# Four consecutive keys per partition: a cache page as 32 rows of 8 KB instead of 128 rows of 2 KB

## What is computed

```python
past_k = cache_k[l][page_table].reshape(dec_batch, past_len, DA_HEADS, 2, DA_HEAD_DIM)
past_v = cache_v[l][page_table].reshape(dec_batch, past_len, DA_HEADS, 2 * DA_HEAD_DIM)

def _da_decode(q, k_new, v_new, past_k, past_v, lam):
    s_past = jnp.einsum("bqhmd,bshmd->bhmqs", q, past_k).astype(jnp.float32)
    s_new = jnp.einsum("bqhmd,bshmd->bhmqs", q, k_new).astype(jnp.float32)
    ...
    a = _diff_map(jnp.concatenate([s_past, s_new], axis=-1), lam).astype(v_new.dtype)
    return (jnp.einsum("bhqs,bshe->bqhe", a[..., :P], past_v)
            + jnp.einsum("bhqs,bshe->bqhe", a[..., P:], v_new))
```

## Time and profile before

| What | Value |
|---|---|
| Median of 3 runs | 1676.59 us (1675.52 to 1678.06) |
| The profiled execution: its own time | 1674.08 us |
| The profiled execution: its span | 1672.5 us |
| Granted TensorE clock, mean of the span | 0.846 |
| DVE STREAM_TRANSPOSE of keys, 32 of them | 72.9 us busy, 48.8 us idle before them |
| PE matmuls for past scores (L1433) | 52.0 us busy, 98.0 us idle before them |
| DMA over the span | 229.19 MB, mean 137 GB/s |
| of it the cache: 128 pages of keys and 128 of values | 256 transfers of 256 KB |

### The profile page before, as it was taken

How to read it: one execution, slowest core, us unless ns; L and a number is a source line. 1 busy time by engine, 2 the same in 40 slices (tenths; PEclk the granted TensorE clock), 3 DMA queues, 4 the chain that set the end, 5 groups by cost and what they waited for, 6 DMA issues and landing times. The chain is left out here.

```text
span 1672.5 us, 25105 instructions
## 1 busy us (share of the span) xinstructions
PE 1186.6 (71%) x9177; PEld 882.0 (53%) x9178; DVE 586.7 (35%) x953; ACT 421.4 (25%) x726; POOL 308.3 (18%) x385
## 2 busy tenths in 40 slices
PE   4799995979797915556055665899418889888960
PEld 3799994868686805445033333677203444344440
DVE  5112012536354465663155553211401121111135
ACT  6101102444444455653011123212000000000120
POOL 4000000000000044342404432221130010000014
PEclk9999997989898956777577877899659999999965
DMA  4422002211112032210969994221054756676248
GB/s 110 101 78 63 13 27 60 71 52 52 57 47 65 27 107 83 83 56 22 326 206 364 385 345 138 78 76 44 20 185 152 273 177 240 246 260 231 81 163 320
DMA packets 149009, 229.19 MB, mean 137 GB/s; under 512 B 16465, under 2 KB 99714, under 8 KB 148930
## 3 DMA queue, kind: packets, MB, share of 16 engines
q1 hardware_dynamic: 121778, 136.33, 25.4%
q0 software_dynamic: 21312, 70.56, 11.8%
q10 hardware_dynamic: 5840, 21.24, 3.2%
HBM read 184.54 MB, written 41.44 MB: 135 GB/s over the span
## 5 line engine op out<-in xcount | busy, mean ns | idle before, releaser
L2066 PE MATMUL ps<-e_ring,e_spare 128*128 x400 | 186.6, 622 | 28.6 <-SPq L1986 28.6
L2066 PEld LDWEIGHTS ps<-e_ring,e_spare 128*128 128x128 f32 x400 | 77.7, 199 | 121.3 <-issue 121.3
L1433 PE MATMUL ps<-d_KT,d_q 32*32 32x512 f32 x1024 | 52.0, 866 | 98.0 <-DVE d_KT L1556 98.0
L2087 PE MATMUL ps<-e_ring,e_hT 128*128 x200 | 92.4, 605 | 19.5 <-ACT e_hT L2127 19.5
L616 PE MATMUL ps<-xh,a_wh 128*128 128x384 f32 (+1 forms) x288 | 101.5, 352 | 0.0
L616 PE MATMUL ps<-xl,a_wh 128*128 128x384 f32 (+1 forms) x288 | 97.3, 338 | 0.0
L616 PE MATMUL ps<-xh,a_wl 128*128 128x384 f32 (+1 forms) x288 | 97.0, 337 | 0.0
L1556 DVE STREAM_TRANSPOSE d_KT<-d_K 128x2048 f32<-128x2048 f32 x32 | 72.9, 2293 | 48.8 <-DMA d_K<-in_cache_k 48.8
L1433 PEld LDWEIGHTS ps<-d_KT,d_q 32*32 32x32 f32 x1024 | 22.2, 128 | 122.5 <-issue 75.9
L2123 ACT ACTIVATE e_sg<-ps 128x256 f32<-128x256 f32 x32 | 12.3, 383 | 282.8 <-PE ps L2066 269.2
L436 PE MATMUL ps<-p_wvl,xh 128*128 128x256 f32 (+1 forms) x288 | 81.3, 282 | 0.0
(11 more groups left out here) (332 smaller groups left out, 2514.8 us busy)
## 6 DMA issues: line engine op xcount, KB each, us to landing
d_V<-in_cache_v POOLq DMA_DIRECT2D x128, 256.0 KB, 7.2
d_K<-in_cache_k SPq DMA_DIRECT2D x128, 256.0 KB, 8.6
e_ring<-in_w_gate SPq DMA_DIRECT2D x16, 1024.0 KB, 6.4
e_ring<-in_w_up SPq DMA_DIRECT2D x16, 1024.0 KB, 11.4
e_ring<-in_w_down SPq DMA_DIRECT2D x16, 1024.0 KB, 13.2
expert_rows<-e_spare ACTq DMA_DIRECT2D x32, 512.0 KB, 2.6
zT<-a_zs POOLq DMA_DIRECT2D x12, 544.0 KB, 3.0
a_w<-in_w_in SPq DMA_DIRECT2D x12, 512.0 KB, 3.8
```

The source lines that it names most:

```text
L1433: ins = pe.matmul(m.ps[32 * h:32 * h + 32, q, :], q4[32 * q:32 * q + 32, j, h, b, :], KT[32 * q:32 * q + 32, 4 * h + j, :, :].rearrange("p ...
L2066: ins = pe.matmul(m.ps[:, 2 + u, :], xgT[:, u, k, :], up_k[:, bass.ds(r * KD + k, 1), :].squeeze(1), start=(k == 0), stop=(k == KD - 1))
L2087: ins = pe.matmul(m.ps[:, 6 + b, :], hT[:, u, f * 128:f * 128 + 128], down_w[:, bass.ds(r * FC + f, 1), b * 512:b * 512 + 512].squeeze(1), ...
```

## The change

Each cache page is seen as 32 rows of four consecutive tokens, 8 KB a row. A page goes to 32 partitions: page j of a group to partitions 32 j to 32 j + 31, for the keys and for the values alike. Four transfers of a group still fill the same bytes of the same tiles, and there are as many transfers as before, of as many bytes. A quarter q of the partitions is now a page of the group instead of a quarter of each page, and the third index of K and V is the token inside a row instead of the page. Keys and values are put down by the same rule, so each weight still meets its value, and nothing else in the code changes: the instructions on PE, DVE and ACT are the same, in the same order, and on SP and POOL only the shape of the transfers differs.

```diff
-        kc = a.cache_k[0, :, :, :, :].rearrange("n p h e -> n p (h e)")
-        vc = a.cache_v[0, :, :, :, :].rearrange("n p h e -> n p (h e)")
+        kc = a.cache_k[0, :, :, :, :].rearrange("n (k j) h e -> n k (j h e)", j=4)
+        vc = a.cache_v[0, :, :, :, :].rearrange("n (k j) h e -> n k (j h e)", j=4)
...
-                    sp.dma_start(K[:, n % KR, j, :], kc[page, :, :]).then_inc(k_in[n % KR], 16)
+                    sp.dma_start(K[32 * j:32 * j + 32, n % KR, :, :].rearrange("p j e -> p (j e)"), kc[page, :, :]).then_inc(k_in[n % KR], 16)
...
-                    pool.dma_start(V[:, b % 2, g * PG + j, :], vc[page, :, :]).then_inc(v_in[b % 2 * NPG + g], 16)
+                    pool.dma_start(V[32 * j:32 * j + 32, b % 2, g * PG:g * PG + PG, :].rearrange("p j e -> p (j e)"),
+                                   vc[page, :, :]).then_inc(v_in[b % 2 * NPG + g], 16)
```

## The result

The changed kernel takes 1761.38 us (median of 4 runs, 1757.59 to 1762.92), the kernel before 1677.32 us beside it: a ratio of 1.0496, with a 95% interval of 1.0472 to 1.0519. It is 5% slower. Forecast were 1744 us, in a range of 1666 to 1802, of which 1701 to 1802 was the likeliest case's own. Spans: 1756.0 us after, 1672.5 us before, so 83.5 us to account for.

A forecast was written before the change was run, and what follows sets the result against it. The decode phase was taken as bound by its key and value transfers. Turns +57 us, start +10 us and end nothing gave +68 us on 1674.1 us, 1742 us, so 1744 us as median; range 1666 to 1802 us.

The forecast's parts named there:

- The bound: Decode phase: key transfer, transpose, scores form the chain; turns of 22.0 us are bound by transfers at 385 GB/s.
- The limit of few partitions: Phase's loads: transfers with few partitions meet a limit in SBUF belonging to the partitions, 217 GB/s in a store of 64.
- Longer rows, best case -9 us: Decode phase: longer rows taken alone raise 385 to 402 GB/s, saving 8 us in 7 turns and 1.2 us in the start.
- How the two streams meet: Keys and values: half the bytes at 217 GB/s in the same half, half at 385 in opposite halves, giving 278 GB/s.
- The turns: Seven turns between the sequences' maxima: 30.2 us each instead of 22.0, +57 us.
- The start: From first key issue to the first sequence's last transpose: 12.7 MB at 278 GB/s take 45.7 us, +10 us.
- The end: Last values of the phase: four groups come 5 us later, but before their use, so it costs nothing.
- Issue on SP: Key transfers: if narrow ones cost SP 598 ns instead of 333, a group is issued 1.1 us later; rival +8.5 us.
- The aligned one: Rival: the free half never helps, both streams bound at 217 GB/s throughout, 1817 us; chance 0.08 for above 1802.
- No limit for loads: Rival: loads meet no partition limit and rows of 8 KB help, -9 us, 1667 us; chance of faster 0.17.
- a row of 8 KB would be cut: Rival: rows of 8 KB are cut into pieces as before; partitions stay few, so no way out of the limit; no own chance.
- the second rival: Prediction's words for the rival whose result would follow if the skill page's ratio alone made 385 into 222 GB/s.

The follow-up runs named there:

- the pinned streams: Changed kernel loading only pages 0 and 1 per group, keys in partitions 0-63, values in 64-127 or also in 0-63: 1653.94 and 1664.46 us.
- the first comparison: Changed kernel with each page on every fourth partition instead of 32 adjacent ones, still rows of 8 KB: 1672.18 us, ratio 0.9950 to the kernel before.

## Why the prediction was right, and where its sizes were off

**The bound.** Right. The phase was paced by its transfers, and their rate decided the result. No engine's instructions changed, and DVE's waits for keys took the loss.

**The limit of few partitions.** Right, and the weakest step of the prediction at that: it went from one pair of stores to loads. The runs on every second partition of a half and on every fourth of the whole show that what counts is whether a transfer reaches both halves.

**Longer rows, best case -9 us.** Right in size, by luck: 9 us between rows of 2 and 8 KB on every fourth partition, and 8 to 9 us against the kernel before. But the prediction had 8 us of it in the turns and 1 in the start. The trace has the start 5.8 us shorter and the turns 2.6 us longer.

**How the two streams meet.** This is the term that was mis-sized. It let opposite halves run at 385 GB/s for half of the bytes, and got 278 GB/s. Measured are 230 to 232, and the pinned streams show 226 GB/s in opposite and 202 in the same half. The prediction would have read such a rate as a badly guessed share of the time in one half. That isn't it: the pinned kernel is in opposite halves all the time, and has no 385. Why a free half is not used stays open. Wide values beside narrow keys at 232 GB/s show that one stream holds up the other; no run shows how.

**The turns.** Forecast +57 us, measured +78. With 230 GB/s, the same sum would be 7 x (36.5 - 22.0) = 101 us, too much: the first two turns took 29.3 and 22.1 us, since their values had been loaded in the start. POOL issues none between 824 and 896 us, and from 860 to 889 us the keys' queue has 88% of the engines' time, the values' 13%. The five others took 36.2 us each, which is 8.39 MB at 232 GB/s. The prediction had seen that values are loaded two sequences ahead, and had not counted it.

**The start.** Forecast +10 us, measured +10.3 at the first maximum, and +11.7 from the first key's issue to the last transpose (35.3 to 47.0 us), which is the stretch that the prediction summed. It is luck, by two errors that cancel. The rate was 232 and not 278 GB/s, at which 12.7 MB would have taken 55 us, but the keys got a larger part of it. From 811 to 840 us, the queues before, and then after:

```profile
q0 software_dynamic: 1986, 6.39, 58.4%
q1 hardware_dynamic: 2600, 4.74, 45.2%
```

```profile
q1 hardware_dynamic: 640, 3.41, 52.4%
q0 software_dynamic: 630, 3.30, 49.8%
```

Before, a packet of keys was 2 KB and one of values mostly two rows, and keys had 4.74 of 11.13 MB, 43%. With 8 KB on both sides they have 51%. The version with 8 KB on every fourth partition also has half of the bytes for keys in this stretch (5.88 of 11.72 MB). Of the 5.8 us by which its first maximum comes early, the higher rate alone (405 against 385 GB/s for 29 us) is some 1.4 us, an estimate; the larger part for keys is the likely rest.

**The end.** Forecast nothing, measured +0.5 us. And behind the phase 5.3 us fell away that the change had no part in, so the whole time flatters the forecast: for the phase, +68 us stand against +88.8.

**Issue on SP.** Wrong for this change:

```profile
L1392 SPq DMA_DIRECT2D d_K<-in_cache_k x128: 315/316/1150, 804.0 to 1061.4; - x128
```

316 ns against 333 before. The 598 ns of the queries' transfers were not the price of few partitions. The prediction kept this out of its sum, as a rival of +8.5 us. Where it said that a later issue is hidden under a full queue, a run bears it out: every second partition of one half takes SP 467 ns an issue, and has the time of the change (1760.55 us).

**The rivals.** The aligned one (1817 us) was nearer in its mechanism than the forecast, since the free half helps by a tenth only. Its time was 56 us too high: 26 us in the two turns that ran on values loaded ahead, 13 in the five others, whose rate was 232 and not 217, some 12 in the start, and the 5 behind the phase. It stands first in the list; where the prediction, beside the ratio of 222 GB/s, speaks of the second rival, this is the one that fits. "No limit for loads" fell with the first comparison. That a row of 8 KB would be cut didn't happen.

## What to carry to other kernels

Before a transfer is made longer by taking fewer partitions, look at which partitions are left: take them with a step over the whole height, not side by side. Here the long rows then cost nothing and gained half a per cent. Where a phase is paced by transfers, read MB and busy share of each queue: a share that stays at 1 while the rate falls from 385 to 232 GB/s, as here, says that each transfer holds its engines longer, though no engine's instructions have changed. And of two streams, the one with the longer packets got the larger part in each run here, so look first at the stream that is waited for; a kernel that gives it the longer packets over the whole height was not measured.

## What the runs showed of the hardware that was not expected

A transfer into one half of the partitions slows transfers that are not confined to that half: values on all partitions fell from 23.6 to 16.3 GB/s an engine beside narrow keys, and the keys and values in opposite halves reached 226 GB/s together, not twice 217.

Pieces of 2 KB that are neighbours in HBM and in the partition were moved in packets of 8 KB, although the transfer was written with rows of 2 KB: 1102 packets for 5.84 MB.

SP's time to issue a transfer of 256 KB depends on its shape: 316 ns for 32 adjacent partitions with 8 KB and 317 ns with four separate rows of 2 KB in each, 333 ns for 128 with 2 KB, 472 ns for 32 at a step of four, 603 ns for those with four separate rows each.
